# Reading direction of TensorE's passes, varied by ring slot in the feature-major stages

## The reference

```
h    = rms_norm(x, ln_pre_mix)
proj = h @ w_in                                   # u | v | q | k | v | gate_a | gate_b
y_a  = gmlp_branch(u, v_sg, ...) @ w_a_out
y_b  = swa_branch(q, k, v, rel_bias, sinks) @ w_b_out
mix  = (gate_a * y_a + gate_b * y_b) @ w_o
x    = x + rms_norm(mix, ln_post_mix)
h2   = rms_norm(x, ln_pre_ffn)
x    = x + rms_norm(conv_ffn(h2, w_up, conv_w, w_down), ln_post_ffn)
```

## Time and profile before

| | |
|---|---|
| median of 3 runs | 1581.42 us (1581.32 to 1582.01) |
| profiled execution | 1581.71 us |
| its span, first to last instruction | 1579.9 us |
| granted TensorE clock, mean | 0.999 |
| PE busy | 1570.8 us |
| DVE busy | 1260.1 us |
| ACT busy | 828.0 us |

### The profile page before, as it was taken

The page is one execution under the profiler, slowest core; times in us unless marked ns, Lnnn a source line. Parts: engine busy times, 40 slices in busy tenths (PEclk is TensorE's granted clock), DMA queues, the critical chain, the costliest instruction groups (busy, mean ns, idle before and its releaser), DMA issues.

```text
span 1579.9 us, 24342 instructions
## 1 busy us (share of the span) xinstructions
PE 1570.8 (99%) x8652; PEld 1361.4 (86%) x8652; DVE 1260.1 (80%) x1836; ACT 828.0 (52%) x1124; POOL 1.9 (0%) x12
## 2 busy tenths in 40 slices
PE   9999999999999999999999999999999999999998
PEld 8888888888888888888888888888888888888886
DVE  6566677677797788777787777877778999989998
ACT  6544544456565654444444444444444575766664
POOL 0000000000000000000000000000000000000000
PEclk9999999999999999999999999999999999999999
DMA  9896455556666465556655566665665655555552
GB/s 370 270 231 194 160 186 166 180 160 206 195 241 218 153 210 189 188 186 204 191 188 188 186 203 190 189 188 186 204 190 188 214 208 205 199 205 195 186 213 107
DMA packets 234946, 313.15 MB, mean 198 GB/s; under 512 B 5360, under 2 KB 209808, under 8 KB 234000
## 3 DMA queue, kind: packets, MB, share of 16 engines
q1 hardware_dynamic: 231056, 306.44, 58.7%
q10 hardware_dynamic: 3840, 6.05, 1.5%
HBM read 309.58 MB, written 2.88 MB: 198 GB/s over the span
## 4 chain that ended last, share of the span: by engine, by line
PE 96%; DVE 4%; issue 0%; ACT 0%; DVEq 0%
PE ps L1493 44%; PE ps L1497 23%; PE ps L1586 15%; PE ps L1779 6%; PE ps L1636 3%; PE ps L1599 1%; DVE actT L1188 1%; DVE w_lo L1188 1%; PE ps L1508 1%; PE ps L1513 0%; DVE arena L1176 0%; PE ps L1725 0%; PE ps L1706 0%; PE ps L1658 0%; PE ps L1718 0%
## 5 line engine op out<-in xcount | busy, mean ns | idle before, releaser
L1493 PE MATMUL ps<-actT,w_hi 128*128 128x512 f32 x3072 | 715.0, 389 | 0.0
L453 ACT ACTIVATE w_hi<-raw 128x1024 fp32r<-128x1024 f32 x420 | 433.2, 1056 | 502.9 <-PE ps L1493 252.0
L861 DVE TENSOR_TENSOR w_lo<-raw,w_hi 128x1024 fp32r<-128x1024 f32 x422 | 506.0, 1222 | 230.8 <-ACT w_hi L453 228.9
L1493 PEld LDWEIGHTS ps<-actT,w_hi 128*128 128x128 f32 x3072 | 569.3, 188 | 112.2 <-issue 0.2
L1497 PEld LDWEIGHTS ps<-actT,w_lo 128*128 128x128 f32 x3072 | 372.4, 188 | 10.2 <-issue 1.7
L1497 PE MATMUL ps<-actT,w_lo 128*128 128x256 f32 x3072 | 378.4, 279 | 0.0
L1586 PE MATMUL ps<-w_hi,xs 128*128 128x512 f32 x832 | 226.6, 389 | 0.0
L1586 PEld LDWEIGHTS ps<-w_hi,xs 128*128 128x128 f32 x832 | 156.1, 188 | 32.5
L1586 PE MATMUL ps<-w_lo,xs 128*128 128x512 f32 x416 | 128.1, 389 | 0.0
L1188 DVE TENSOR_TENSOR w_lo<-raw,w_hi 128x1024 fp32r<-128x1024 f32 x96 | 116.7, 1215 | 0.0
L1378 DVE SCALAR_TENSOR_TENSOR arena<-arena,convw 128x256 f32<-128x256 f32 x256 | 106.7, 479 | 0.0
(11 more groups left out here) (181 smaller groups left out, 933.6 us busy)
## 6 DMA issues: line engine op xcount, KB each, us to landing
raw<-in_w_up_dram SPq DMA_DIRECT2D x128, 1024.0 KB, 5.4
raw<-in_w_down_dram SPq DMA_DIRECT2D x64, 1024.0 KB, 5.3
raw<-in_w_in_dram SPq DMA_DIRECT2D x58, 1024.0 KB, 5.2
raw<-in_w_o_dram SPq DMA_DIRECT2D x16, 1024.0 KB, 5.3
raw<-in_w_a_out_dram SPq DMA_DIRECT2D x8, 1024.0 KB, 5.2
raw<-in_w_b_out_dram SPq DMA_DIRECT2D x8, 1024.0 KB, 5.3
arena<-in_x_dram SPq DMA_DIRECT2D x1, 2048.0 KB, 16.8
arena<-in_x_dram ACTq DMA_DIRECT2D x2, 1024.0 KB, 6.2
```

What stands on the lines that cost most here:

```text
L453: act.activation(w_hi[:, h % RING, :], raw[:, h // 2, h % 2 * HALF:(h % 2 + 1) * HALF], ACT.Copy)\
L861: dve.tensor_tensor(lo, raw[:, h // 2, h % 2 * HALF:(h % 2 + 1) * HALF], w_hi[:, h % RING, :].bitcast(F32), ALU.subtract).then_inc(lo_read ...
L1493: return pe.matmul(ps[:, bank + c, :], w_hi[:, h % RING, at:at + P], actT[:, k, :, :].rearrange("p a s -> p (a s)"), start=start, stop=stop)
```

## The change

The direction of a pass now depends on the ring slot of its half, by a new function `by_turns`:

- narrow passes in slot 0: reversed for column block c = 1;
- narrow passes in slot 1: reversed for odd k;
- wide passes in slot 2: reversed for column block c = 1;
- wide passes in slot 3: reversed for odd k.

Wide passes in slots 0 and 1 and narrow ones in slots 2 and 3 stay as they were. Reversed means that moving operand and output are both gone over with a step of -1, so that each product lands where it did. The step of the last narrow pass of a run is multiplied with this one: in slot 1 the two cancel, which is where k is odd and `wide_next` holds.

```diff
--- before.py
+++ after.py
@@ -1489,11 +1489,16 @@
 
         @block.tensor
         def _(pe):
+            def by_turns(slot, first, k, c):
+                return -1 if slot == first and c == 1 or slot == first + 1 and k % 2 == 1 else 1
+
             def by_hi(h, at, k, c, bank, start, stop):
-                return pe.matmul(ps[:, bank + c, :], w_hi[:, h % RING, at:at + P],
-                                 actT[:, k, :, :].rearrange("p a s -> p (a s)"), start=start, stop=stop)
+                step = by_turns(h % RING, 2, k, c)
+                return pe.matmul(ps[:, bank + c, ::step], w_hi[:, h % RING, at:at + P],
+                                 actT[:, k, :, :].rearrange("p a s -> p (a s)")[:, ::step], start=start, stop=stop)
 
             def by_lo(h, at, k, c, bank, start, stop, step=1):
+                step *= by_turns(h % RING, 0, k, c)
                 return pe.matmul(ps[:, bank + c, 0:S][:, ::step], w_lo_shifted[h % RING][:, at:at + P],
                                  actT[:, k, 0, ::step], start=start, stop=stop)
```

## The result

The kernel became slower, by 1.3%. Before, the median was 1581.59 us (1581.32 to 1582.01), after it 1601.76 us (1601.60 to 1602.04), four runs each; the ratio is 1.0127 (95% interval 1.0115 to 1.0139), or 20.2 us.

A forecast was written before the change was run, and what follows sets the result against it. TensorE's matmuls, busy 1570.8 of 1579.9 us, bound the kernel. The profiled 1581.71 us + 0 + 0 + 0.1 gave 1581.8, or 1581.5 us for the median; range 1572 to 1592 us for 8 in 10.

The forecast's parts named there:

- the sum's two zeros: In the changed TensorE passes: 0 for reversing a pass and 0 for each change of direction between passes.
- A reversed pass by itself: 1536 reversed TensorE passes: 0 each; loss at most 8 ns wide, 4 ns narrow; gain at most 13.3 and 9 ns.
- A turn of direction: 2304 direction changes in TensorE's runs: 0 each; gain up to 14 ns, loss up to 13 ns wide, 10 ns narrow.
- the turns breaking a settled rhythm: Slower rival: direction changes unsettle TensorE's pitch, each paying part of an entry; 6.6 us, up to 26 us; chance 0.30.
- the small rivals: TensorE's changed passes: slower by direction changes, 6.6 us (0.30), or faster by meeting the weight load less, 5.7 us (0.24).
- What would show it: Group turn runs stay 7.26 and 3.71 us; if rhythm breaks, slots by c lose twice those by k; otherwise both alike.
- The faster rival: Reversed TensorE passes meet the weight load less, saving a third of their overhead: 5.7 us, 1576 us; chance 0.24.
- The much slower rival: Wide passes with output step -1 take twice their 226.7 ns: 174 us more, 1756 us; chance 0.03.
- TensorE's passes go to the end one for one: What a TensorE pass gains or loses reaches the end fully, while a turn stays above about 17 us.
- The 0.11 us for the 8 places in the y turns: Last narrow passes of pairs in slots 0 and 1 turn forward again; 14 ns each, 0.11 us lost.

The follow-up runs named there:

- uniform kernel: The changed kernel with all wide passes in slots 2 and 3 and all narrow ones in slots 0 and 1 reversed; 1599.1 us.
- the kernel with islands: The changed kernel with one reversed pass of eight in slots 2 (wide) and 0 (narrow), two in a row in slots 3 and 1; 1595.1 us.
- one turn in the half: The changed kernel with four forward, then four reversed passes in each half of the changed slots, 768 turns in place of 2304; 1595.5 us.

## Why the prediction was wrong

**The step that failed** is the sum's two zeros, "A reversed pass by itself" and "A turn of direction". The median came out 20.2 us above before, outside the range of 1572 to 1592. It is in the case that had 0.30, the turns breaking a settled rhythm. That mechanism is there, but it is only a part, and the case's own size for it (6.6 us) was three times too small; that reading backwards costs by itself was in none of the small rivals. So the case was hit in part by luck.

**A reversed pass by itself, taken as 0.** It costs 6.7 ns wide and 4.4 ns narrow once settled (uniform kernel), against bounds of 8 and 4 ns. At 768 passes of each kind these two are 8.5 us, which is far over the 3.2 that tell a change. The row that the zero stood on could not have shown it. It has 120 ns from 377.31 to 377.43; the trace's start times, in whole ns, give 117 for this pass and for the last narrow pass of every pair in the y stage, and in the kernel with no reversed pass the same places take 116 or 117. So 120 was the view's rounding, and one reversed pass at the end of a forward run is not a settled one: its near-zero price says nothing of runs that are full of them.

**A turn of direction, taken as 0.** If each reversed pass is given its settled price, the other 11.7 us of the change lie here, the 4.8 us in unchanged slots among them. The same estimate gives 9.9 us for 768 turns in the kernel with islands (13 ns a turn), 4.9 us for 768 in that with one turn in the half (6 ns), 11.7 us for 2304 in the change (5 ns), and nothing for the uniform kernel, where it hides the 2.3 us of the slots behind. So a turn has no fixed price, and no run separates the two terms inside a mixed run: the changed slots of the change go at the pitch of the uniform kernel (233.6 against 233.5 ns, 119.6 in both). What is shown is that for wide passes the return to forward costs most, 17 to 42 ns by how many reversed passes stood before it.

The argument against this rival was that the reversed pass before a wide run goes with the smaller entry, 13 against 27 ns. In kind this was right: without these passes the kernel takes 1.9 us more, with the shift unchanged, and the entry is about 26 ns in place of 1 in the looped turns and 47 in place of 13 in the y stage. But that was a turn at a change of width, and I carried it over to turns between equal passes, where the sign is the other one.

**What would show it.** The test that I had set, by c against by k, doesn't separate the two. The slots by c and by k lose nearly the same in wide passes (5.0 and 5.2 us), which would say "the reversed pass", and by k loses more in narrow ones (3.3 against 1.8), though it has half the turns. It left out that a slot hands its state to the next: slots 0 (wide) and 2 (narrow), with not one changed pass, lost 4.7 us. The run of 32 passes does show the loss.

**The faster rival** falls: between equal passes no reversed pass in place of a forward one gave time, except with unshifted narrow weights, 118.3 against 120.0 ns, and that is still above 115.6. **The much slower rival** falls: writing backwards costs nothing. What held is that TensorE's passes go to the end one for one (20.1 us in the changed lines, 0.2 less elsewhere, 19.9 of span), that the others follow, and that nothing else moves. The 0.11 us for the 8 places in the y turns can't be told in the runs; by the entries of 47 and 13 ns in that stage it would be 0.27 us, small as well.

**What stays open.** The cost is on the side of the reading of the moving operand, and for narrow passes its sign turns with the start of the weights; so it seems that what counts is how the reading and the weight load lie to each other, which is argued and not shown. No simple rule for it survived: not the length of the load, not the place of the start within 16 bytes, not the direction alone. A reversed weight load was not tried. Why runs that change direction after every pass or two go at the pitch of reversed ones is not known. Why a pass of 496 columns leaves its run settled and one of 256 doesn't is not known either. No version here beats the kernel before.

## What to carry to other kernels

Where TensorE is busy for 99% and passes follow each other without a gap, measure the pitch from start to start, in tenths of a ns and by place in the loop; the durations in the groups of the profile show only a hint of it, and no wait will. In this kernel equal passes settle to a steady pitch, and a pass that reads in another way than the one before it can cost the next two to nine; a single one is worth placing with care (here before a change of width), many are not. A zero that a change multiplies by a thousand needs a row that can tell a few ns: here the view rounded to 10 ns and showed one pass where the change makes 1536, and it took the uniform kernel, a run full of them, to show the price.

## What was not expected of the hardware

- The direction in which the moving operand is read matters, that of the output doesn't (as far as it was tried, in whole runs): 233.3 against 226.7 ns for 512 columns and 120.0 against 115.6 for 256, and 1582.2 us with only the output reversed.
- A disturbance outlives its cause by two to nine passes. After the change, slot 0's forward passes take 230.5 233.3 235.8 224.2 230.8 235.8 228.3 232.4 ns and the next 230.7 before the pitch is 226.7 again; some of them are shorter than the settled pitch.
- With wide passes reversed in turn, one of two or two of four, the pitch is that of runs read backwards throughout: 233.6 against 233.5 ns on the mean.
- Moving the start of the weights by 8 bytes takes 4.4 ns off a narrow forward pass, adds 4 ns to a wide forward one and leaves a wide reversed one where it is.
- "TensorE: Matmul & The Clock Gate" of the Trainium skill, part 2, has two independent read ports and N / 2.4 + 2.5 ns from pass to pass (215.8 for 512 columns). The runs here disagree with the pitch, 226.7 ns settled. That the pitch also depends on where the weights start (120.0 or 115.6 ns for 256 columns) speaks against ports that don't touch each other, though no run here shows the ports themselves.
